# Prompt attention placed between the key chunks of sample attention in a two-layer decoder step on Trainium2

## The chip, the cores and the metric

The kernel runs on one core of a Trainium2 chip. A core has a matrix engine (PE, TensorE) with its weight loads (PEld), a vector engine (DVE), a scalar engine (ACT), GpSimd (POOL), a queue engine (SP), and 16 DMA engines. The engines run side by side, each through its own list of instructions in order, and wait for one another by semaphores. The metric is the device time of one execution in microseconds (us). All data are float32.

## The reference, cut to what matters

One inference step of two layers for a prompt of 512 tokens and, with the same weights, a sample group of 8 sequences with 4 new tokens each and 2048 past positions. In each layer:

```
x = x + 0.5 * SwiGLU_1(RMSNorm(x))
h = RMSNorm(x); z = h @ w_in             split into the heads of A, B and C
A: gated DeltaNet, 4 heads of 128
B: dilated sliding-window attention, 4 heads of 64, branches (128,1), (512,4), (2048,16)
C: differential attention, 4 heads: (softmax1 - lambda * softmax2) @ v, two 32-wide maps, 64-wide values
x = x + concat[A | B | C] @ w_out
x = x + 0.5 * SwiGLU_2(RMSNorm(x))
```

The prompt attends to itself (causal). For the samples C reads 2048 past keys and values per sequence from a paged pool by a page table, and B reads those of a window cache that its branches touch (896 of 2048 rows). A relative bias is added to every logit. Beside the outputs the step returns the new states, keys and values.

## The kernel before, in words

Activations stand transposed: 128 features on the partitions, 544 columns of tokens (512 prompt, 32 sample). A layer runs in stages: first FFN, input projection (`project`), DeltaNet for the prompt in four chunks (`chunk`) and for the samples (`sample_chunk`), `sample_attention`, `prompt`, output projection (`w_out`), second FFN. Each engine's order is written out by hand in its own block, and each block has a function of the same name for a stage; `s[...]` are semaphores, counted up over both layers. PSUM has 8 banks of 512 columns.

**Sample attention** (PE L908, ACT L1345, DVE L1928) goes through 46 key chunks of 512 KB (128 partitions x 4 rows x 256). Chunks 0 to 31 are of C, four sequences each in groups g = 0 and 1, gathered by POOL with indirect DMAs (`load_k`, L530); chunks 32 to 45 are of B, loaded by SP in four DMAs each. The ring for keys has 4 slots, and so has the ring for values (`load_v`, L538). Per chunk PE turns 8 blocks of 128 x 128 into banks 4 and 5 (`turn_keys`), ACT copies bank 4 (L1347) and DVE bank 5 (L1953) to the double-buffered `kt`, and PE multiplies the queries with it (`scores(n - 1)`, one chunk behind). The scores of a group fill banks 0 to 3; every fourth chunk DVE adds the bias and takes a partial maximum (`logits_c`). After 16 chunks follow the group's maximum, exponentials on ACT (`exp_c`), and weights: 17 matmuls of the exponentials with a matrix `comb`, which turn, normalise and combine the two maps (`weights_c`, L962). Then come the group's 16 value chunks, one per key chunk (`value`, L974), into banks 6 and 7; for group 0 from step 21, for group 1 from step 39, and its last ones after the key loop. `sums` (L994) collects the values over partitions. At the end B's window has its logits, maximum, exponentials, a diagonal matrix, weights and 16 value loads by SP.

**Prompt attention** (PE L1055, ACT L1390, DVE L2042) starts when DVE has copied out the samples' results. It has 16 units u: two heads times 128 queries, against 128 * (u % 4 + 1) keys; units 0 to 7 are of B with one map, 8 to 15 of C with two (`maps`). A unit is: scores (PE, L1067), logits with bias (DVE, L2051), maximum (L2056) and its negative (L2058), exponentials with row sums (ACT, L1398), reciprocals and weights (DVE, L2064 to L2075), turn of the weights (PE, `turned`, by the helper at L575), copy `p_pt` (ACT), values (PE, L1088), result (DVE, L2080). Engines work one to three units apart: PE's iteration u has scores of u + 1, turn of u - 1 and values of u - 2. Tiles and banks are those that sample attention has left: `p_s` and `p_pt` lie in `arena`.

**What stands around it.** SP loads the first two output-weight slots (L475, 1 MB each, into `weight_slots`) right after the input projection, then the four sample states (L370, needed by PE at L884), then B's keys and values. POOL writes out the four new sample states (L511) and then starts the gathers. The output projection (L1108) waits for the last prompt result, with all sample results in place before.

## Time and profile before

| | us |
|---|---|
| median of 3 runs | 3529.67 |
| lowest, highest | 3528.74, 3530.52 |
| the profiled execution | 3515.54 |
| its span, first to last instruction | 3513.9 |
| PE busy | 3117.7 (89%) |
| PEld busy | 2498.4 (71%) |
| DVE busy | 1597.9 (45%) |
| ACT busy | 623.5 (18%) |
| POOL busy | 143.8 (4%) |
| mean granted TensorE clock | 0.91 |

The profile is of one execution. A row of the timeline gives start and length in us, the engine, the line of the kernel, the operation with written and read tiles, a count if several were merged, and in brackets how long the engine had stood idle and what ended that.
### The profile page before, as it was taken

How to read it: one execution, taken by the hardware profiler on the slowest of the kernel's cores; microseconds unless marked ns; L12 is line 12 of the kernel's file. 1: busy time of each engine (PE TensorE's matmuls, PEld its weight loads, DVE VectorE, ACT ScalarE, POOL GpSimd, SP SyncE). 2: the span in 40 equal slices, each digit the busy share in tenths (PEclk: the TensorE clock that was granted, in tenths of full speed). 3: DMA queues.
4: the chain of work that ended last, by engine and by line, in shares of the span. 5: the costliest groups of instructions: out<-in, count | busy, mean ns of one | idle time of the engine just before them, and what ended most of it. 6: DMA issues, size and time to landing. Idle time of an engine off the chain costs nothing.

```text
span 3513.9 us, 46297 instructions
## 1 busy us (share of the span) xinstructions
PE 3117.7 (89%) x16564; PEld 2498.4 (71%) x16564; DVE 1597.9 (45%) x2966; ACT 623.5 (18%) x1233; POOL 143.8 (4%) x164
## 2 busy tenths in 40 slices
PE   2999999988887688999979999999878876899996
PEld 1788877877654366888868888788775534688885
DVE  3544535345443545445354454443554246444443
ACT  0111001233231321110011100122332213111100
POOL 0000000000052000000000000000003200000000
PEclk7999999999788588999989999999987867999998
DMA  4222232220079112221232212221005850232221
GB/s 142 61 84 72 66 90 60 66 70 0 27 270 268 39 60 60 84 84 57 75 87 84 84 57 78 69 72 60 28 27 181 242 153 1 84 84 84 60 75 59
DMA packets 363619, 299.01 MB, mean 85 GB/s; under 512 B 19426, under 2 KB 334972, under 8 KB 363170
## 3 DMA queue, kind: packets, MB, share of 16 engines
q1 hardware_dynamic: 340060, 213.88, 21.2%
q0 software_dynamic: 21888, 78.85, 6.7%
q10 hardware_dynamic: 1520, 4.27, 0.3%
q8 instruction: 94, 1.54, 0.2%
q14 instruction: 57, 0.47, 0.0%
HBM read 285.15 MB, written 11.81 MB: 85 GB/s over the span
## 4 chain that ended last, share of the span: by engine, by line
PE 80%; DVE 7%; DMA 6%; DVEq 2%; issue 2%; ACT 1%; ACTq 1%; SPq 1%; POOL 0%; POOLq 0%
PE banks L616 28%; PE banks L672 16%; PE banks L728 12%; PE banks L639 4%; PE banks L575 3%; PE banks L1108 3%; PE banks L802 1%; PE banks L810 1%; PE banks L814 1%; DMA hidden_or_projected<-in_cache_k,layer_cache_rows 1%; DMA arena<-in_cache_v,layer_cache_rows 1%; DMA arena<-in_cache_win_v 1%; DMA hidden_or_projected<-in_cache_win_k 1%; DVE arena L2056 1%; PE banks L904 1%
## 5 line engine op out<-in xcount | busy, mean ns | idle before, releaser
L728 PE MATMUL banks<-normed_or_mixed,weight_slots 128*128 128x272 f32 x1792 | 417.5, 395 | 10.5 <-DVE normed_or_mixed L1552 10.5
L728 PEld LDWEIGHTS banks<-normed_or_mixed,weight_slots 128*128 128x128 f32 x1792 | 343.0, 192 | 83.4 <-DVE normed_or_mixed L1552 12.0
L616 PE MATMUL banks<-arena 128*128 128x272 f32 x1408 | 347.8, 401 | 15.2 <-DVE arena L1577 15.2
L616 PE MATMUL banks<-normed_or_mixed,arena 128*128 128x272 f32 x1408 | 337.0, 392 | 0.0
L616 PEld LDWEIGHTS banks<-arena 128*128 128x128 f32 x1408 | 274.1, 195 | 76.0 <-DVE arena L1577 17.7
L616 PEld LDWEIGHTS banks<-normed_or_mixed,arena 128*128 128x128 f32 x1408 | 267.5, 190 | 55.1
L575 PE MATMUL banks<-constants,hidden_or_projected 128*128 128x128 f32 (+2 forms) x880 | 132.4, 300 | 61.8 <-DMA hidden_or_projected<-in_cache_k,layer_cache_rows 21.7
L672 PE MATMUL banks<-hidden_or_projected,keys_values_by_token 128*128 128x272 f32 x704 | 177.0, 392 | 0.0
L575 PEld LDWEIGHTS banks<-constants,hidden_or_projected 128*128 128x128 f32 (+2 forms) x880 | 105.6, 153 | 95.6 <-issue 78.1
L672 PE MATMUL banks<-hidden_or_projected,weight_slots 128*128 128x272 f32 x704 | 169.2, 392 | 0.0
L672 PE MATMUL banks<-arena,keys_values_by_token 128*128 128x272 f32 x704 | 169.2, 392 | 0.0
L575 PE MATMUL banks<-constants,arena 128*128 128x128 f32 (+4 forms) x306 | 62.2, 355 | 107.5 <-DVE arena L2075 46.0
L672 PEld LDWEIGHTS banks<-hidden_or_projected,keys_values_by_token 128*128 128x128 f32 x704 | 133.8, 190 | 27.6
L672 PEld LDWEIGHTS banks<-hidden_or_projected,weight_slots 128*128 128x128 f32 x704 | 133.8, 190 | 27.6
L672 PEld LDWEIGHTS banks<-arena,keys_values_by_token 128*128 128x128 f32 x704 | 133.8, 190 | 27.6
L1596 DVE TENSOR_TENSOR arena<-arena,banks 128x272 f32<-128x272 f32 x88 | 38.5, 437 | 249.9 <-PE banks L616 249.9
L639 PE MATMUL banks<-normed_or_mixed,keys_values_by_token 128*128 128x272 f32 x384 | 103.2, 415 | 43.5 <-DVE normed_or_mixed L1552 43.5
L1956 DVE COPY hidden_or_projected<-banks 128x512 f32<-128x512 f32 x92 | 63.6, 691 | 170.8 <-PE banks L575 170.7
L575 PEld LDWEIGHTS banks<-constants,arena 128*128 128x128 f32 (+4 forms) x306 | 44.7, 175 | 134.4 <-DVE arena L2075 57.6
L1179 ACT ACTIVATE arena<-banks 128x256 f32<-128x256 f32 (+7 forms) x164 | 83.0, 513 | 273.0 <-PE banks L802 107.2
L1108 PE MATMUL banks<-normed_or_mixed,weight_slots 128*128 128x272 f32 x512 | 122.0, 401 | 7.3 <-DVE normed_or_mixed L2131 6.3
L1734 DVE COPY hidden_or_projected<-banks 128x544 f32 x28 | 20.3, 724 | 222.7 <-PE banks L728 222.7
(365 smaller groups left out, 4631.0 us busy)
## 6 DMA issues: line engine op xcount, KB each, us to landing
weight_slots<-in_w_down SPq DMA_DIRECT2D x128, 256.0 KB
weight_slots<-in_w_in SPq DMA_DIRECT2D x28, 1024.0 KB
keys_values_by_token<-in_w_gate SPq DMA_DIRECT2D x48, 512.0 KB, 4.7
keys_values_by_token<-in_w_up SPq DMA_DIRECT2D x48, 512.0 KB, 4.7
weight_slots<-in_w_gate SPq DMA_DIRECT2D x40, 512.0 KB, 5.0
weight_slots<-in_w_up SPq DMA_DIRECT2D x40, 512.0 KB, 5.1
hidden_or_projected<-in_cache_win_k SPq DMA_DIRECT2D x112, 128.0 KB, 8.2
weight_slots<-in_w_down SPq DMA_DIRECT2D x64, 192.0 KB
```

Of the source, the lines that this page charges most:

```text
L575: return pe.transpose(out, in_, ident[0:rows, 0:rows])
L616: mm = pe.matmul(ps[:, bank, 0:HALF], weights[:, k, :], acts[:, k, :], start=first and k == 0, stop=k == 3, skip_group_check=True)
L639: mm = pe.matmul(ps[:, c, 0:HALF], one[:, k, :], hT[:, k, left], start=k == 0, stop=k == 3, skip_group_check=True)
L672: mm = pe.matmul(ps[:, bank, 0:HALF], weights[:, 128 * k:128 * k + 128], acts[:, k, :], start=j == 0 and k == 0, stop=j == 2 and k == n - 1)
L728: mm = pe.matmul(half(bank + 2 * u, h), wslot[:, slot, at:at + 128], hT[:, k, h * HALF:(h + 1) * HALF], start=k == 0, stop=k == KD - 1)
L802: mm = pe.matmul(ps[:, 4 if a else 7, 128 * i:128 * i + 128], m["LK"][:, 2 * a + i, :], m["T"][:, 2 * a + i, :], start=True, stop=True)
L810: mm = pe.matmul(ps[:, 2 + a, 128 * i:128 * i + 128], m["U"][:, 2 * a + i, :], m["M"][:, 2 * a + i, :], start=True, stop=True)
L814: mm = pe.matmul(ps[:, 5 + a, 128 * i:128 * i + 128], m["M"][:, 2 * a + i, :], m["U"][:, 2 * a + i, :], start=True, stop=True)
L1108: mm = pe.matmul(half(2 * (o % 4), h), wslot[:, o // 2 % 2, at:at + 128], hT[:, k, h * HALF:(h + 1) * HALF], start=k == 0, stop=k == KD - 1)
L1179: return act.activation(out, in_, ACT.Copy, scale=scale)
L1596: dve.tensor_tensor(x, one, a, ALU.add).then_inc(s["mix_out"], 1)
L1956: cp(kt[:, n % 2, 1, :], ps[:, 5, :]).then_inc(s["kt_v"], 1)
```

## The change

`sample_attention` and `prompt` become one function, `attention`, on each engine. The 46 key chunks are 46 steps, and after the samples' own work each step does a part of a prompt unit: `unit_at` gives units 0 to 7 two steps each (steps 0 to 15), units 8 to 15 three each (16 to 39); part 0 and 1 score the maps, the exponentials and weights of a unit come in the step after its last scores (part `maps(u)`), its turn in part 0 of the next unit and its values in part 1.

What else changes:
- ACT copies both banks of turned keys in one copy of 1024 columns; DVE's key copies are gone, with the signals `k_half`, `kt_a` and `kt_v`.
- Banks: turned keys 0 and 1, sample scores 2 only (four chunks at a time, so DVE's logits come every fourth chunk for B too), new scores and values 3, prompt scores 4 and 5, turned weights and results 6 and 7. DVE takes the maximum over all 2080 columns at once, without partial maxima.
- Group 0's values run in steps 20 to 35, copied out in two halves; group 1's in steps 38 to 45, two chunks per step, none after the loop. The sums of both groups come together after the windows' weights.
- `p_s` moves to the tile of the weight slots; so SP's first two output-weight loads move behind the last prompt turn and the first four window-value loads.
- POOL issues the first four key gathers before the four state stores.
- The output projection and the squares before it wait for the last sample results.

```diff
-        vblk = carve(work, 0, 8, 128)[0], carve(work, 1024, 8, 128)[0]
+        vblk = carve(work, RING * 1024, 8, 128)[0], carve(work, RING * 1024 + 1024, 8, 128)[0]
...
-        p_s, at = carve4(arena, 0, 2, 2, 2, SEQ)
-        p_pt, at = carve4(arena, at, 2, 2, 4, 128)
+        p_s, _ = carve4(raw[1], 0, 2, 2, 2, SEQ)
+        p_pt, _ = carve(work, 20 * NT, 2, 4, 128)
...
+        def unit_at(step):
+            if step < 16:
+                return step // 2, step % 2
+            return 8 + (step - 16) // 3, (step - 16) % 3
...
 @block.sync
-                for slot in range(2):
-                    sp.wait_ge(s["proj_done"], l * 28 + 26 + 2 * slot)
-                    load_wide(l, "w_out", slot * 256, slot)
                 sp.wait_ge(s["state_done"], l * 5 + 5)
...
                 for m in range(2 * NB_S):
+                    if m == RING:
+                        sp.wait_ge(s["ppt_mm"], l * 16 + 16)
+                        for slot in range(2):
+                            load_wide(l, "w_out", slot * 256, slot)
...
 @block.gpsimd
-                for h in range(NH):
-                    gp.wait_ge(s["st_new"], l * 4 + h + 1)
-                    st(O["delta_s"][ds(l, 1), :, h].rearrange("l b k v -> k (l b) v"), t["st"][:, h], "st_out")
...
+                gp.wait_ge(s["x_act"], l * 5 + 1)
+                for n in range(RING):
+                    load_k(n)
+                for h in range(NH):
+                    gp.wait_ge(s["st_new"], l * 4 + h + 1)
+                    st(O["delta_s"][ds(l, 1), :, h].rearrange("l b k v -> k (l b) v"), t["st"][:, h], "st_out")
+                for n in range(RING, CH_C):
                     load_k(n)
...
 @block.tensor
+                def prompt_scores(u, mp):
+                    hp, q0, wid = u // 4 % 2, 128 * (u % 4), 128 * (u % 4 + 1)
+                    if u:
+                        pe.wait_ge(s["p_log"], l * 24 + map_of(u, mp))
...
+                def prompt_turn(u):
+                    pe.wait_ge(s["p_soft"], l * 16 + u + 1)
+                    if u >= 1:
+                        pe.wait_ge(s["p_out"], l * 16 + u)
+                    if u in (8, 14):
+                        pe.wait_ge(s["pt_sb"], l * 3 + 1 + u // 14)
...
+                def prompt_step(step):
+                    u, part = unit_at(step)
+                    if part == 0:
+                        if u < 16:
+                            prompt_scores(u, 0)
+                        if 0 < u <= 16:
+                            prompt_turn(u - 1)
+                    if part == 1:
+                        if 8 <= u < 16:
+                            prompt_scores(u, 1)
+                        if 0 < u <= 16:
+                            prompt_values(u - 1)
...
+                for n in range(CH_K):
                     turn_keys(n)
+                    if n == 19:
+                        weights_c(0, 8)
+                    if n == 37:
+                        weights_c(1, 14)
+                    if n:
+                        scores(n - 1)
+                    if 20 <= n < 36:
+                        value(0, n - 20)
+                    if n >= 38:
+                        value(1, 2 * n - 76)
+                        value(1, 2 * n - 75)
+                    prompt_step(n)
...
 @block.scalar
                 def keys(n):
-                    act.wait_ge(s["k_half"], k_seen(l, n))
+                    act.wait_ge(s["k_free"], k_seen(l, n) + RING)
                     act.wait_ge(s["ks_mm"], l * CH_K + n + 1)
-                    copy(kt[:, n % 2, 0, :], ps[:, 4, :]).then_inc(s["kt_a"], 1)
+                    copy(kt[:, n % 2].rearrange("p a n -> p (a n)"), flat[:, 0:1024]).then_inc(s["kt_sb"], 1)
...
+                def prompt_step(step):
+                    u, part = unit_at(step)
+                    if u < 16 and part == maps(u):
+                        wid = 128 * (u % 4 + 1)
+                        act.wait_ge(s["p_max"], l * 16 + u + 1)
...
+                for n in range(CH_K):
+                    keys(n)
+                    if n in (17, 33):
+                        exp_c(n // 16 - 1)
...
+                    prompt_step(n)
...
 @block.vector
-                def keys(n):
-                    dve.wait_ge(s["k_free"], k_seen(l, n) + RING)
-                    dve.wait_ge(s["ks_mm"], l * CH_K + n + 1)
-                    cp(kt[:, n % 2, 1, :], ps[:, 5, :]).then_inc(s["kt_v"], 1)
...
                 def max_c(g):
                     dve.drain()
-                    dve.reduce_max(c_mx[:, g, 0:1], c_mx[:, g, 4:9], AX)
+                    dve.reduce_max(c_mx[:, g, 0:1], c_s[g][:, :], AX)
...
+                for n in range(CH_K):
...
+                    if 4 <= n <= CH_C and n % 4 == 0:
+                        logits(n // 4 - 1, n)
+                    if n == 40:
+                        logits(8, n)
+                    if n in (16, 32):
+                        max_c(n // 16 - 1)
+                    if n in (18, 34):
+                        comb_c(n // 16 - 1)
+                    prompt_step(n)
```

## Rows read from the trace of the kernel before

**Rows 1.** The chain that ended last, share of the span by engine (the page, part 4).

```profile
PE 80%; DVE 7%; DMA 6%; DVEq 2%; issue 2%; ACT 1%; ACTq 1%; SPq 1%; POOL 0%; POOLq 0%
```

**Rows 2.** Timeline: start us, length us, engine, line, operation. The stage's borders in both layers.

```profile
983.59 1.96 PE L575 MATMUL banks<-constants,hidden_or_projected 128*128 128x128 f32 x8 [2.30 <-ACT keys_values_by_token L1452]
...
1112.24 0.65 PE L958 MATMUL banks<-hidden_or_projected,arena 128*32 128x128 f32 x16
...
1167.11 2.98 PE L1067 MATMUL banks<-hidden_or_projected 64*128 64x128 f32 x12 [0.89 <-DVE normed_or_mixed L2038]
...
1260.24 5.76 PE L1108 MATMUL banks<-normed_or_mixed,weight_slots 128*128 128x272 f32 x24 [0.47 <-DVE normed_or_mixed L2080]
...
2680.03 1.96 PE L575 MATMUL banks<-constants,hidden_or_projected 128*128 128x128 f32 x8 [2.31 <-ACT keys_values_by_token L1452]
...
2967.64 5.76 PE L1108 MATMUL banks<-normed_or_mixed,weight_slots 128*128 128x272 f32 x24 [0.47 <-DVE normed_or_mixed L2080]
```

**Rows 3.** Stretches: us; PE, PEld, DVE, ACT, POOL busy; clock, DMA share, GB/s.

```profile
986.00:1028.00 42.00, 34.41 (x496) 25.87 (x496) 20.35 (x39) 14.91 (x23) 22.24 (x24) 0.95 0.81 286
...
1131.50:1167.10 35.60, 29.36 (x177) 11.71 (x176) 9.91 (x12) 1.94 (x2) 0.00 (x0) 0.53 0.58 177
...
1194.00:1254.00 60.00, 32.34 (x196) 20.87 (x194) 46.32 (x98) 26.26 (x77) 0.00 (x0) 0.62 0.00 1
```

**Rows 4.** Timeline, PE: one step with keys, scores and a value chunk.

```profile
1035.28 1.09 PE L575 MATMUL banks<-constants,hidden_or_projected 128*128 128x128 f32 x8
...
1037.31 1.09 PE L575 MATMUL banks<-constants,hidden_or_projected 128*128 128x128 f32 x8
```

**Rows 5.** Groups by form in layer 0's sample attention: count | busy us, mean ns | idle before.

```profile
L1179 ACT ACTIVATE hidden_or_projected<-banks 128x512 f32<-128x512 f32 x46 | 27.4, 596 | 82.1 <-PE banks L575 82.1
...
L1179 ACT ACTIVATE arena<-banks 128x1024 f32<-128x1024 f32 x6 | 6.0, 1022 | 38.3 <-PE banks L1049 27.6 <-PE banks L971 10.5 <-PE banks L990 0.2
...
L1956 DVE COPY hidden_or_projected<-banks 128x512 f32<-128x512 f32 x46 | 31.8, 691 | 79.9 <-PE banks L575 79.8
```

**Rows 6.** Timeline: exponentials of a narrow two-map unit, then logits to weights of a wide one.

```profile
1226.78 0.40 ACT L1398 ACTIVATE arena<-arena 128x128 f32<-128x128 f32 x1 [1.10 <-DVE arena L2058]
...
1243.83 2.35 DVE L2051 SCALAR_TENSOR_TENSOR arena<-banks,prompt_bias 128x1024 f32<-128x1024 f32 x2 [0.99 <-PE banks L575]
...
1246.27 2.29 DVE L2056 TENSOR_REDUCE arena<-arena 128x4 f32<-128x2048 f32 x1
...
1248.84 0.72 ACT L1398 ACTIVATE arena<-arena 128x512 f32<-128x512 f32 x1 [4.51 <-DVE arena L2058]
...
1251.16 1.54 PE L575 MATMUL banks<-constants,arena 128*128 128x128 f32 x6 [6.84 <-DVE arena L2075]
...
1251.80 0.18 DVE L2064 RECIPROCAL arena<-arena 128x4 f32<-128x4 f32 x1 [0.49 <-ACT arena L1398]
...
1253.15 1.41 DVE L2075 SCALAR_TENSOR_TENSOR arena<-arena 128x512 f32<-128x512 f32 x2
```

**Rows 7.** Timeline, PE: values of the widest unit and of the narrowest.

```profile
1189.28 1.09 PE L1088 MATMUL banks<-arena,keys_values_by_token 128*64 128x128 f32 x16
...
1193.17 0.44 PE L1088 MATMUL banks<-arena,keys_values_by_token 128*64 128x128 f32 x4
```

**Rows 8.** DMA issues of the stage: count, median us from issue to landing.

```profile
arena<-in_cache_v,layer_cache_rows POOLq DMA_INDIRECT x32, 7.2
```

**Rows 9.** Timeline: sample weights, the windows' diagonal, and 32 sums of values.

```profile
1090.07 3.76 PE L969 MATMUL banks<-arena 128*128 128x64 f32 x32
...
1116.99 0.29 DVE L2027 TENSOR_SCALAR arena<-constants,arena 128x128 f32<-128x128 f32 x1
...
1159.24 6.98 PE L1001 MATMUL banks<-constants,arena 128*128 128x16 f32 x32 [2.15 <-ACT arena L1179]
```

**Rows 10.** Stretches (columns as in rows 3): the state loads.

```profile
924.00:928.00 4.00, 4.00 (x39) 3.27 (x37) 0.89 (x6) 0.00 (x0) 0.00 (x0) 0.68 1.01 304
```

**Rows 11.** Timeline, PE: the products with the loaded states.

```profile
935.75 13.82 PE L884 MATMUL banks<-arena 128*128 128x8 f32 x64 [0.45 <-ACT arena L1179]
```

More of the change, by code:

```diff
@@ new lines, in prompt_turn @@
+                def prompt_turn(u):
[4 more added lines that the diff above has]
+                        pe.wait_ge(s["pt_sb"], l * 3 + 1 + u // 14)
+                        alone(pe)
+                    for kb in range(u % 4 + 1):
+                        cols = slice(128 * kb, 128 * kb + 128)
+                        for h2 in range(2):
+                            mm = turn(ps[:, 6 + h2, cols], p_s[:, u % 2, 0, h2, cols])
+                    mm.then_inc(s["ppt_mm"], 1)
@@ new lines, in prompt_values @@
+                def prompt_values(u):
+                    pe.wait_ge(s["ppt_sb"], l * 16 + u + 1)
+                    for kb in range(u % 4 + 1):
+                        for h2 in range(2):
+                            v0 = 128 * (u // 4) + 64 * h2
+                            mm = pe.matmul(ps[64 * h2:64 * h2 + 64, 6, 0:128], vtok[:, kb, v0:v0 + 64],
+                                           p_pt[:, h2, kb, :], start=kb == 0, stop=kb == u % 4)
+                    mm.then_inc(s["po_mm"], 1)
@@ L1152, in _ @@
                 alone(pe)
-                sample_attention(l)
-                prompt(l)
+                attention(l)
                 w_out(l)
@@ L1385, in sample_attention @@
-                values_c(1)
-                act.wait_ge(s["v_free"], l * 48 + 48 + RING)
-                copy(pv_b[:, 0:4, :], flat[:, 0:1024].rearrange("p (b n) -> p b n", b=4))
-                copy(pv_b[:, 4:8, :], flat[:, 3072:4096].rearrange("p (b n) -> p b n", b=4)).then_inc(s["pv_sb"], 1)
-            def prompt(l):
-                for u in range(17):
-                    if u < 16:
+                    copy(c_pt[:, g, 0:16, :], flat[:, 3072:4096].rearrange("p (k n) -> p k n", k=16))
@@ new lines, in prompt_step @@
+                def prompt_step(step):
+                    u, part = unit_at(step)
+                    if part == 0 and 2 <= u <= 8:
+                        prompt_result(u - 2)
+                    if part == 2 and 8 <= u <= 16:
+                        prompt_result(u - 1)
+                    if u < 16 and part < maps(u):
+                        prompt_logits(u, part)
+                        if part == maps(u) - 1:
+                            prompt_max(u)
+                    if u < 16 and part == maps(u):
+                        prompt_weights(u)
@@ new lines, in attention @@
+                for n in range(CH_K):
+                    if n == 2:
+                        dve.wait_ge(s["st_out"], l * 64 + 64)
+                        alone(dve)
+                        for g in range(2):
+                            new_logits(g, c_s[g][:, PAST:PAST + NS], scale_c, bias_cn[:, g, :])
+                        new_logits(2, b_s[:, KEYS_B:KEYS_B + NS], scale_b, bias_bn[:, :])
+                    if 4 <= n <= CH_C and n % 4 == 0:
[7 more added lines that the diff above has]
+                    prompt_step(n)
@@ new lines, in attention @@
+                for i in range(2):
+                    norm_a(i)
+                out_c()
+                for i in range(2, 4):
+                    norm_a(i)
+                dve.wait_ge(s["pv_mm"], l * 2 + 2)
+                for pair in range(2):
+                    for h2 in range(2):
+                        rows = slice(64 * h2, 64 * h2 + 64)
+                        at = 16 * pair + 4 * (2 * pair + h2)
+                        last = cp(hT[rows, 4 + pair, SEQ:NT].rearrange("p (b t) -> p b t", b=8),
+                                  ps[rows, 3, 0:256].rearrange("p (b x) -> p b x", b=8)[:, :, at:at + 4])
@@ L2091, in _ @@
+                last.then_inc(s["pv_out"], 1)
             with dve.Fori(0, DEPTH) as l:
@@ L2125, in _ @@
                 dve.drain()
-                sample_attention(l)
-                prompt(l)
+                attention(l)
                 for u in range(2):
```

363 lines of the change are left out of this document (129 added, 234 removed).

## The prediction

> **What bounds the kernel now.** I read first the chain that ended last: PE carries 80% of it [rows 1], so a change pays where PE is late or waits, and not where ACT or DVE is merely busy. Then I placed the changed stage by the timeline [rows 2]: in layer 0 the first key turn starts at 983.59 us, the last sample scores of the windows end at 1112.9, the prompt's first scores start at 1167.11 and the output projection at 1260.24. That is 276.7 us: 129.3 for 46 key chunks, 54.2 for the end of sample attention, 93.1 for the prompt. In layer 1 the same stage takes 287.6 us (2680.03 to 2967.64). Third, the busy time by stretches [rows 3]: over 42 us of the key chunks PE is busy 34.4 at clock 0.95, the 16 DMA engines are 81% busy, DVE is busy half the time and ACT a third; over 60 us of the prompt PE is busy 32.3, DVE 46.3, the DMAs nothing, and the clock is 0.62, that is, three quarters of it at the 1.2 GHz level. So one half of the stage leaves DVE and ACT free and the other leaves PE and the DMAs free; the change lays the one into the other.
>
> **What one step costs.** A step with keys, scores and one value chunk takes 2.03 us at the full clock (1035.28 to 1037.31) [rows 4]. Until now ACT and DVE each copied one bank of turned keys; now ACT alone copies both. 46 x 0.69 = 31.8 us leave DVE, and ACT's 27.4 us become 46 x 1.02 = 47 us [rows 5]. PE's turn of the next chunk waits for that copy: 1.09 + 1.02 and two hand-overs of 0.1 make 2.3 us the least step, hidden where the step's other PE work is longer.
>
> **Steps 0 to 15** (units 0 to 7, two steps each). PE has per unit 2 x (1.09 + 0.65) and gaps of 0.8, that is 4.3, and the unit's scores, turns and values: turns and values 1.09 each for the widest unit and 0.44 for the narrowest [rows 4, 7], the scores taken alike, so with the two widths between 3.1 for each kind over four units. Four units are 4 x 4.3 + 9.3 = 26.5, eight are 53, with the three products of new keys 55 us. Maxima, exponentials and weights of these one-map units are shorter (about 5 us even for the widest) and lie beside PE.
>
> **Steps 16 to 39** (units 8 to 15, three steps each). Here a ring of engines is longer than PE's work. From the end of one turn to the end of the next, widest unit: keys, scores and value of the next step 2.4 with gaps, scores of map two 1.1, their logits 1.2 (half of 2.35), maximum 2.3 and its sign 0.3, exponentials 3.0 (1248.84 to 1251.80), weights 2.8 (1251.80 to 1254.56) [rows 6], and the turn of the unit before, 0.9: 14.1 us with a hand-over or two. Narrowest: 2.4, scores 0.5, then not DVE's 1.5 but PE's old values, next turn and ACT's copy, 3.5, exponentials 1.7 (four of 0.39 and a read), weights 1.6, turn 1.1: 10.8 [rows 5 to 7]. By the same steps the two between take 10.4 and 12.0. Four units are 47.3, eight 95 us. Queued into that ring: the two sets of sample weights (17 matmuls, 3.8 us each on PE [rows 9] in front of a turn that also waits for ACT's copy; half is hidden, 4 us), and the maximum over 2080 columns, now taken at once (2.3 us by the widths of rows 6), with its exponential in ACT's queue ahead of a prompt unit, 3 us. 102 us.
>
> **Steps 40 to 45**, with two value chunks each. PE needs 3.9 us per step, but a step moves 1.57 MB, 5.5 us at the 286 GB/s of rows 3, and a value gather takes 7.2 us (median) to land in a ring of four [rows 8]. I take 32 us, near the transfers.
>
> **The end.** Before: 54.2 us. Window logits, maximum, exponential and diagonal took 4.4 (1112.9 to 1117.3) and take 4.1 with half of the logits done in step 40. Then come the weights, 3.8 as for the samples' and no longer behind late value chunks, the sums of both groups together, 7.0 [rows 9], and the window values with the last copies and sums, 35.6 at clock 0.53 [rows 3]. With 1.5 for hand-overs 52 us.
>
> **What moves for nothing.** Two loads of output weights, 2.1 MB or 7.3 us of transfer, go behind four window-value loads on SP. They pass 4 state loads, 56 window-key issues and 4 value issues. The wait on the last prompt turn ahead of them is over since step 40; behind it queue 12 value loads, first needed 15 us later, and that gap is the cover: without it, 7 us per layer. On POOL four key gathers pass the four state stores; their issue takes about 5 us from 924, and no store can start before PE's state products end at 949.6 [rows 11]. Fewer small maxima and one signal instead of two cost DVE nothing.
>
> **What moves at a price.** Those four gathers (2.1 MB) now start at 924, with the state loads, which fill the DMA engines over 924 to 928 (share 1.01) [rows 10]; PE needs the states at 935.75 [rows 11]. Bounds: 0 if the states go first, 3 us per layer if the two share alike (4.2 MB at 286 GB/s end at 938.7). I take 1, since the state loads are issued first. The Trainium skill (DMA: Bandwidth & Descriptors, the part on queues and rings) says that each engine takes packets from its queues in turn; by that rule it is the upper end, and the sum would be 4 us longer over two layers.
>
> **The clock.** The counts above are at the full clock. The key loop has 0.95, the prompt 0.62 [rows 3]. Between them I take 0.92, as PE is busy about 80% of the new ring: 16% of 189 us at the half level, where PE's work takes double, 15 us. Best 5 (clock 0.97), worst 70 (clock 0.62, all on the path).
>
> **The sum.** 55 + 102 + 32 + 52 + 15 + 1 = 257 us per layer, against 276.7 and 287.6: 19.7 and 30.6 less, 50 us in all. The profiled execution took 3515.54 us (span 3513.9, 1.6 around it), so it would take 3465; the median of the runs is 14.1 us higher, and from there it is 3480.
>
> **Rivals.**
> (a) *The ring runs clean.* Clock 0.97 and the last steps at PE's 23 us instead of 32: 257 - 10 - 9 = 238 per layer, 88 less: 3441. For it: at 82% busy PE kept 0.95. Against: the new ring leaves PE idle for 2 to 3 us in its wide units, which the key loop seldom does.
> (b) *The half clock.* Place: PE standing in front of the turn of a wide two-map unit until DVE's weights are done, about 3 us of idle time, eight units per layer. At clock 0.62 the sum is 257 - 15 + 70 = 312: 35 and 24 longer, 3589. It turns the sign where the clock costs 40 us instead of 15, a loop clock of about 0.79. For it: the prompt's own rows, where PE stood up to 6.8 us in front of such a turn [rows 6]. Against: now keys and values fill most of them. The Trainium skill (TensorE: Matmul & The Clock Gate, on oscillation) says that bursts of matmuls parted by waits fall back to the half clock again and again; by that rule it is this rival, and the prompt's rows agree while the key loop's don't.
> (c) *Nothing is hidden.* ACT works in order: a key copy stands behind exponentials, these behind a maximum, and each engine waits for the next, so that the prompt keeps its 93 us and the longer copies add 46 x 0.42 = 19 per layer: 3529.7 + 39 = 3568. Against: PE turns one chunk ahead of that copy.
> (d) *The transfers bound it.* 48 MB a layer (by the sizes of the chunks) at 286 GB/s are 168 us, below my 189 + 52, so this is only a floor and gets no chance.
>
> **How the numbers follow.** Forecast 0.50, (a) 0.22, (b) 0.14, (c) 0.14. The likeliest case's own range is 3455 to 3515 (10 us a layer on the ring, 5 on its last steps and the clock). Both signs hold weight, so the range reaches over (a) to 3435 and toward (c) to 3550; above it lie (b) and most of (c). 0.2% or 7 us is what a measurement of this kernel can tell. Faster: (a) and all but 0.02 of the forecast, 0.70. Slower: 0.24 of the 0.28 of (b) and (c), since a weak form of either ends at no change. Same: the 0.06 that is left.
>
> **What would show it.** In the timeline of the changed kernel: from the first key turn to the output projection 257 us in each layer; the 16th key turn 55 us after the first; from there to the 40th 102 us, with 14 us between the turns of the widest units; a full-clock step of 2.3 us where nothing of the prompt is in it; state products still starting at 936; clock over the loop at 0.92. Wrong if the narrow units also take 14 us (c), if the clock of the loop is below 0.8 (b), or if PE waits mostly for DMA in steps 16 to 39.

## The result and the profile after

The changed kernel takes 3425.62 us (median; 3424.5 to 3428.39), the kernel before took 3529.2 beside it: ratio 0.9707, 95% interval 0.969 to 0.9724, **103.6 us faster**. The forecast was 3480 and the range began at 3435. Direction right, gain twice what I said.

The profiled executions differ by less: 3515.54 before, 3428.39 after, 87.2 us by their spans. The page of the changed kernel, busy time by engine and, further down, the chain that ended last:

```profile
PE 3095.6 (90%) x16564; PEld 2494.0 (73%) x16564; DVE 1534.9 (45%) x2854; ACT 658.0 (19%) x1237; POOL 145.0 (4%) x164
...
PE 83%; DVE 7%; DMA 3%; ACT 2%; issue 2%; DVEq 2%; ACTq 1%; SPq 0%; POOL 0%; POOLq 0%
```

PE does almost the same busy time in a span 87 us shorter, and its share of the chain goes from 80% to 83%, DMA's from 6% to 3% [rows 1]. Line numbers have moved: L586 is the turn helper, L963 the sample scores, L997 the values, L1019 the prompt scores, L1111 the output projection. Timeline of PE, the stage's borders in layer 0 (first key turn, 17th, 41st, last scores, output projection), then layer 1's first and last:

```profile
991.66 1.97 PE L586 MATMUL banks<-constants,hidden_or_projected 128*128 128x128 f32 x8
...
1037.36 1.09 PE L586 MATMUL banks<-constants,hidden_or_projected 128*128 128x128 f32 x8
...
1141.42 1.09 PE L586 MATMUL banks<-constants,hidden_or_projected 128*128 128x128 f32 x8
...
1170.91 0.61 PE L963 MATMUL banks<-hidden_or_projected,arena 128*32 128x128 f32 x16
...
1222.56 3.08 PE L1111 MATMUL banks<-normed_or_mixed,weight_slots 128*128 128x272 f32 x6 [0.97 <-DVE normed_or_mixed L2080]
...
2650.61 1.97 PE L586 MATMUL banks<-constants,hidden_or_projected 128*128 128x128 f32 x8
...
2877.35 3.08 PE L1111 MATMUL banks<-normed_or_mixed,weight_slots 128*128 128x272 f32 x6 [0.96 <-DVE normed_or_mixed L2080]
```

The stage takes 230.9 and 226.7 us instead of 276.7 and 287.6 [rows 2]. The same pieces as in the sum of the prediction:

| piece, us | forecast | layer 0 | layer 1 |
|---|---|---|---|
| steps 0 to 15 | 55 | 45.7 | 45.7 |
| steps 16 to 39 | 102 | 104.1 | 100.7 |
| steps 40 to 45 and the last scores | 32 | 30.1 | 30.5 |
| end | 52 | 51.0 | 50.0 |
| clock, over all steps | 15 | in the above | in the above |
| state loads | 1 | (outside) | (outside) |
| sum | 257 | 230.9 | 226.7 |

The same pieces by stretches: from shortly before step 3's key turn to step 15, 16 to 39, 40 to 45, the end, and last steps 16 to 39 of layer 1 (us; PE, PEld, DVE, ACT, POOL busy; clock, DMA share, GB/s):

```profile
1000.00:1037.36 37.36, 35.05 (x453) 25.16 (x445) 22.51 (x54) 25.45 (x48) 16.64 (x18) 1.00 0.77 250
1037.36:1141.42 104.06, 88.02 (x1000) 60.19 (x999) 50.36 (x97) 52.67 (x102) 28.60 (x31) 0.92 0.72 209
1141.42:1171.50 30.08, 23.93 (x290) 15.63 (x286) 4.31 (x11) 10.81 (x17) 9.99 (x10) 0.83 0.89 275
1171.50:1222.56 51.06, 42.43 (x230) 22.64 (x227) 21.25 (x25) 4.68 (x9) 0.00 (x0) 0.52 0.58 168
...
2696.27:2796.92 100.65, 84.79 (x1000) 58.67 (x999) 50.39 (x97) 52.67 (x102) 28.74 (x31) 0.95 0.73 217
```

In the first piece PE is busy 94% at the full clock. In the second it is busy 85%, and DVE and ACT half the time each. What PE waits for there (engine, line, releaser: us in total, times, longest):

```profile
PE banks L586 <- DVE weight_slots L2024: 6.4, 4, 3.0
PE banks L586 <- DVE normed_or_mixed L2029: 4.0, 1, 4.0
PE banks L993 <- ACT hidden_or_projected L1181: 3.8, 1, 3.8
PE banks L586 <- ACT hidden_or_projected L1181: 1.0, 2, 0.5
PE banks L586 <- ACT arena L1181: 0.3, 1, 0.3
```

That is 15.5 of PE's 16.0 idle us: nine short waits for DVE and ACT, none for DMA. In the key loop of the kernel before PE waited 21.1 us for keys and values, here 3.5 us in all 46 steps of layer 0.

Of the 106.7 us that the stage saves (45.8 + 60.9), 19.5 are **given back** outside it: 8.1 ahead of layer 0's first key turn (983.59 to 991.66), 8.3 between the layers, 3.1 at the end. Two places can be read off; start, length, operation and idle time before it:

```profile
940.31 4.87 PE L895 MATMUL banks<-arena 128*128 128x8 f32 x22 [2.42 <-DMA arena<-in_state_delta]
...
990.65 1.08 PE L944 MATMUL banks<-hidden_or_projected,arena 128*32 128x32 f32 x64 [5.66 <-DVE arena L1944]
```

The state products wait 2.42 us for their loads (2.28 in layer 1), before 0.45 for ACT [rows 11]. And the scores of the new keys, which need DVE's `q_all`, now stand ahead of the first key turn, so PE waits 5.66 us where it waited 2.30 [rows 2]. A third is the output projection after layer 0, which comes out of a stretch at clock 0.52: its first 24 products take 8.63 us, before 5.76 [rows 2]. These three make 2.9 + 3.4 + 1.8 = 8.1 of the 8.3 us between the layers; Of layer 0's 8.1 us 2.6 lie ahead of the state products. 1.6 of them are already there at a product of the input projection (748.82 after, 747.19 before), whose place varies from 747.30 to 750.71 in the versions below though the code up to it is the same; 0.9 arise between that product and the samples' DeltaNet, in layer 0 only, and their cause is open. Of the 3.1 us at the end 1.5 are the output projection of layer 1, whose first 24 products take 7.28 us.

### The profile page after: what moved, and what is told of

It is laid out like the page before. It is cut to its first block, busy times and chain, and to the rows that moved or that the text cites. A ratio compares the mean times of both kernels' runs of the same rounds, so it can differ in the third digit from the quotient of the medians.

```text
span 3426.7 us, 45921 instructions
## 1 busy us (share of the span) xinstructions
PE 3095.6 (90%) x16564; PEld 2494.0 (73%) x16564; DVE 1534.9 (45%) x2854; ACT 658.0 (19%) x1237; POOL 145.0 (4%) x164
## 4 chain that ended last, share of the span: by engine, by line
PE 83%; DVE 7%; DMA 3%; ACT 2%; issue 2%; DVEq 2%; ACTq 1%; SPq 0%; POOL 0%; POOLq 0%
PE banks L627 29%; PE banks L683 16%; PE banks L739 12%; PE banks L650 4%; PE banks L586 4%; PE banks L1111 3%; PE banks L813 2%; PE banks L821 1%; PE banks L825 1%; ACT weight_slots L1376 1%; PE banks L963 1%; PE banks L915 1%; PE banks L1008 1%; PE banks L895 1%; DVE normed_or_mixed L1551 1%
## 5 line engine op out<-in xcount | busy, mean ns | idle before, releaser
L739 PEld LDWEIGHTS banks<-normed_or_mixed,weight_slots 128*128 128x128 f32 x1792 | 343.6, 192 | 83.6 <-DVE normed_or_mixed L1551 12.1
L1181 ACT ACTIVATE hidden_or_projected<-banks 128x1024 f32<-128x1024 f32 (+3 forms) x160 | 137.3, 864 | 243.6 <-PE banks L586 163.2
L586 PE MATMUL banks<-constants,hidden_or_projected 128*128 128x128 f32 (+2 forms) x880 | 136.8, 309 | 28.6 <-DMA hidden_or_projected<-in_x_sample 12.1
L586 PEld LDWEIGHTS banks<-constants,hidden_or_projected 128*128 128x128 f32 (+2 forms) x880 | 113.8, 160 | 48.3 <-issue 20.3
L1111 PE MATMUL banks<-normed_or_mixed,weight_slots 128*128 128x272 f32 x512 | 127.7, 414 | 8.3 <-DVE normed_or_mixed L2123 6.4
L1111 PEld LDWEIGHTS banks<-normed_or_mixed,weight_slots 128*128 128x128 f32 x512 | 103.0, 202 | 32.0 <-DVE normed_or_mixed L2123 7.2
L650 PEld LDWEIGHTS banks<-normed_or_mixed,keys_values_by_token 128*128 128x128 f32 x384 | 76.8, 201 | 64.3 <-DVE normed_or_mixed L1551 48.2
L1207 ACT ACTIVATE arena<-banks 128x272 f32<-128x272 f32 x88 | 34.9, 397 | 343.3 <-PE banks L650 343.1
```

The lines of the kernel that those rows point to most:

```text
L586: return pe.transpose(out, in_, ident[0:rows, 0:rows])
L650: mm = pe.matmul(ps[:, c, 0:HALF], one[:, k, :], hT[:, k, left], start=k == 0, stop=k == 3, skip_group_check=True)
L739: mm = pe.matmul(half(bank + 2 * u, h), wslot[:, slot, at:at + 128], hT[:, k, h * HALF:(h + 1) * HALF], start=k == 0, stop=k == KD - 1)
L1111: mm = pe.matmul(half(2 * (o % 4), h), wslot[:, o // 2 % 2, at:at + 128], hT[:, k, h * HALF:(h + 1) * HALF], start=k == 0, stop=k == KD - 1)
L1181: return act.activation(out, in_, ACT.Copy, scale=scale)
L1207: act.activation(p_one[:, g, :], ps[:, 3 * g, 0:HALF], ACT.Copy).then_inc(s["one_done"], 1)
```

## The experiments

Twelve kernels, in three groups of four with the kernel before beside each. Ratios are to that one; the changed kernel's own is 0.9707. Equal code differs between layers and runs: steps 16 to 39 take 100.7 to 104.1 us (mean 102.1; the changed kernel and the three whose edits lie outside, two layers each), the end 46.7 to 51.0. The clock of those eight stretches of steps 16 to 39 differs too, and with it goes the time: 104.1 us at 0.92, 102.1 to 103.2 at 0.93, 100.7 and 100.8 at 0.95. A piece is compared with these spreads.

**Prompt steps behind the key loop** (`e1_serial`).

```diff
                         value(1, 2 * n - 76)
                         value(1, 2 * n - 75)
+                for n in range(CH_K):
                     prompt_step(n)
```

(PE's part; ACT and DVE have the same. On PE the sample weights no longer wait for prompt results, ACT's last value copy comes ahead of its prompt steps, and DVE gets a wait of its own for the new scores.)

> The changed kernel with all 46 prompt steps taken out of the key loop and put behind it, in the same order; banks, single key copy, two values per step and the late sums stay. If laying the prompt into the key loop brings the gain: the stage (first key turn to output projection) is the bare loop, about 46 x 2.6 = 120 us, the prompt's old 93 and the end's 51, that is 264 against the 231 and 227 measured with the change: 33 to 37 more per layer, about 3495 us in all. Rival, that the rest of the change (one copy, group 1's values inside the loop, sums taken together) brings most of it: at most 10 more per layer, under 3446.

Measured 3639.34 us, ratio 1.0315 (1.029 to 1.0339): 214 us slower than the changed kernel and slower than the kernel before. Stretches: steps 0 to 15, 16 to 39, 40 to 45, then the prompt alone:

```profile
990.80:1029.70 38.90, 29.16 (x376) 21.69 (x368) 2.46 (x6) 16.39 (x16) 18.16 (x20) 0.89 0.74 246
1029.70:1119.80 90.10, 74.47 (x814) 52.85 (x814) 9.37 (x13) 33.06 (x35) 28.76 (x31) 0.81 0.81 243
1119.80:1149.00 29.20, 23.17 (x234) 12.63 (x230) 0.69 (x1) 6.16 (x7) 9.36 (x10) 0.71 0.89 253
1149.00:1280.00 131.00, 75.19 (x364) 41.82 (x368) 66.21 (x144) 40.11 (x114) 0.00 (x0) 0.54 0.07 21
```

Neither theory had this. The prompt part alone takes 131 us, not 93: PE waits 36.5 us for DVE's weights of two-map units, up to 8.2 us at a time. By the code the reason is that there is one bank pair for scores, one `p_pt` and one result bank, where the kernel before had two of each; no run takes these apart. The bare loop takes 158 us, before 129.3 (part of it eight value chunks that came later): PE's key turns wait 11.8 us for ACT's copy of both banks, before 1.2 us, and the clock is 0.81 and 0.71 there. Placed in the loop, the prompt costs 179.8 - 158.2 = 22 us. So the new layout makes each part slower on its own, by 38 and 29 us (the 29 with the eight chunks), and placing one in the other hides 109 of 131. It also keeps the clock up: 0.81 without the prompt in steps 16 to 39, 0.92 with it.

**Each prompt maximum twice** (`e2_max_twice`).

```diff
                     dve.reduce_max(p_mx[:, par, 0:2 * n], rows, AX)
+                    dve.drain()
+                    dve.reduce_max(p_mx[:, par, 0:2 * n], rows, AX)
```

> DVE takes each prompt maximum twice. Theory A, a ring of engines sets steps 16 to 39: all of the second maxima of the two-map units (0.69, 1.22, 1.75, 2.29 us, twice, 11.9) lie on it: 12 us more per layer there, 0 to 2 in steps 0 to 15, about 3450 us. Theory B, PE's own list sets them and only its few waits for DVE's weights (four in layer 0, 6.4 us) count: the repeats of just those units, about 6 per layer, 3438 us. If DVE is hidden altogether: 3426.

Measured 3478.36 us, ratio 0.9868 (0.9848 to 0.9888): 26 per layer. Steps 0 to 15 take 50.4, steps 16 to 39 121.7 and 120.7:

```profile
1040.90:1162.60 121.70, 98.39 (x1001) 68.08 (x999) 60.92 (x106) 53.07 (x102) 28.57 (x31) 0.82 0.61 179
```

DVE is busy 10.6 us more there and the stretch is 17.6 and 20.0 longer. The clock falls as well, from 0.92 and 0.95 to 0.82 and 0.84, and PE's busy time grows by 10.4 us in layer 0, so the 17.6 can't be divided for certain between DVE's work and PE's slower products. For a ring (theory A) speaks which units get longer: the rounds from one unit's turn to the next grow by 0.8 to 6.3 us, in all eight units of layer 1 and in seven of layer 0, not just in the four where PE had waited (theory B). Both theories missed the size, 12 and 6 us against 26 per layer, since neither had the clock, and steps 0 to 15 grow by 4.7 where A gave them 0 to 2.

**The sample score products twice** (`e3_scores_twice`).

```diff
-                    for pair in range(2):
-                        for b4 in range(4):
+                    for twice in range(2 if n < CH_C else 1):
+                        for pair in range(2):
+                            for b4 in range(4):
...
```

> PE does the sample score products of chunks 0 to 31 twice, 0.57 us more per chunk at the full clock. Both theories: 9 us more per layer in steps 0 to 15, where PE is busy 94%. Steps 16 to 32: theory A (ring), one of a unit's three scores lies on the ring, 3 us; theory B (PE's list), all of it, 9 us. Sum A 12 per layer, 3450 us; B 18 per layer, 3462 us.

Measured 3440.63 us, ratio 0.9763 (0.9743 to 0.9783). The added products are cheaper than I wrote: 32 instead of 16 records take 1.01 us to the next start where 16 took 0.57, so 0.44 per chunk. Steps 0 to 15 take 50.8 and 50.9, 5.1 more of 15 x 0.44 = 6.6: mostly PE's list, as both theories say. Steps 16 to 39 hold 17 x 0.44 = 7.5 of them (B) and take 106.1 and 104.6, 4.0 and 2.5 above the mean of equal code and 2.0 and 3.9 above the changed kernel's layers; A's share is 0.44 per unit of the first six, 2.6. Stretch of steps 16 to 39:

```profile
1040.20:1146.30 106.10, 94.24 (x1274) 67.87 (x1270) 50.75 (x97) 52.57 (x102) 28.43 (x31) 0.92 0.73 205
```

PE is busy 6.2 us more there, for 2 to 4 us of time, at clocks of 0.92 and 0.93. That is nearer to A's 2.6 than to B's 7.5: in steps 16 to 39 added work of PE costs a quarter to a half of its length, where DVE's 10.6 us above came with 17.6 and more.

**Two engines copy the turned keys** (`e4_two_copies`).

```diff
-                    copy(kt[:, n % 2].rearrange("p a n -> p (a n)"), flat[:, 0:1024]).then_inc(s["kt_sb"], 1)
+                    copy(kt[:, n % 2, 0, :], ps[:, 0, :]).then_inc(s["kt_sb"], 1)
```

```diff
                 for n in range(CH_K):
+                    dve.wait_ge(s["k_free"], k_seen(l, n) + RING)
+                    dve.wait_ge(s["ks_mm"], l * CH_K + n + 1)
+                    cp(kt[:, n % 2, 1, :], ps[:, 1, :]).then_inc(s["kt_v"], 1)
```

> The changed kernel with the copy of the turned keys divided as before: ACT one bank, DVE the other (0.60 and 0.69 us instead of 1.02 on ACT alone). Theory A: DVE's copies stand in the ring of the two-map units, one or two per unit, 8 us more per layer in steps 16 to 39, nothing in steps 0 to 15: 3442 us. Theory B: PE never waits long for the copy (2.1 us in all), so no change, 3422 to 3428. Below that if the single copy was a cost that the ring hid.

Measured 3431.9 us, ratio 0.9731 (0.9711 to 0.9751). Steps 0 to 15 take 47.6, 1.9 more in both layers, and steps 16 to 39 take 103.6 in both, inside the spread. Both expectations miss: the cost is where PE is busiest and not in the ring. In steps 0 to 15 of layer 0 PE waits 2.7 us for DVE's copies (seven times, up to 0.6 us), where it waited 1.1 us for ACT's. In steps 16 to 39 it waits 8.9 us for them, and less for DVE's weights (1.6 us instead of 6.4), so there the wait changed its place. The single copy brings about 2 us per layer in steps 0 to 15; the intervals of the two ratios overlap.

**Key gathers behind the state stores** (`e5_gathers_last`).

```diff
-                gp.wait_ge(s["x_act"], l * 5 + 1)
-                for n in range(RING):
-                    load_k(n)
                 for h in range(NH):
...
+                for n in range(RING):
+                    load_k(n)
```

> The changed kernel with POOL's first four key gathers back behind the four state stores. If the gathers ahead of the stores slow the state loads: the state products (L895 of the changed kernel) start without the 2.4 us wait for DMA in layer 0, and layer 1 likewise: up to 2.4 us less per layer, 3421 us. Rival: the gathers then land too late (the last is issued at 981 and takes 7 us, first key turn at 991.7, so 3 us to spare) and PE waits for keys in its first steps: 0 to 3 us more per layer, up to 3432 us. No change if the two cancel.

Measured 3415.8 us, ratio 0.9688 (0.9671 to 0.9705). The state products start without a wait for DMA:

```profile
937.58 12.75 PE L894 MATMUL banks<-arena 128*128 128x8 f32 x59 [0.45 <-ACT arena L1180]
```

and no turn of gathered keys waits for DMA, although the first four gathers are issued at 978 to 983; steps 0 to 15 take 44.8, 0.9 less, at clock 0.97 instead of 0.91. So the gathers ahead of the stores cost about 3 us per layer and bring nothing: 2 are the wait for the states, and why steps 0 to 15 gain too wasn't traced.

**Value copies one step earlier** (`e6_copies_early`).

```diff
-                    if n in (28, 36):
-                        values_c(0, (n - 28) // 8)
+                    if n in (27, 36):
+                        values_c(0, (n - 27) // 8)
...
-                    if n == 42:
+                    if n == 41:
                         values_c(1, 0)
```

> ACT copies out the first half of each group's values one step earlier (steps 27 and 41 instead of 28 and 42), ahead of a wide unit's four exponentials instead of behind them. PE stood 3.8 us in step 28 and 1.1 us in step 42 for these copies. Theory A (ring): the exponentials of unit 11 start when DVE's maximum is ready, so the copy moves into ACT's idle time; the wait goes, but the ring's next turn is at most 1 to 3 us earlier, since it waits for DVE's weights: 1 to 3 us less per layer, 3421 us. Theory B (PE's list): all 4.9 us per layer, 3416 us.

Measured 3425.19 us, ratio 0.9717 (0.9701 to 0.9734): no change. PE's timeline shows where the wait went:

```profile
1087.64 0.61 PE L993 MATMUL banks<-keys_values_by_token,arena 32*32 32x256 f32 x2
...
1092.82 1.97 PE L586 MATMUL banks<-constants,weight_slots 128*128 128x128 f32 x8 [3.58 <-DVE weight_slots L2024]
```

In the changed kernel PE stood 3.78 us in front of L993 and turned unit 11's weights at 1093.76 with no wait. Now it stands 3.58 in front of the turn, at 1092.82. The wait moved down the ring, as A says, but A's gain of 1 to 3 us isn't there.

**Idle products ahead of the waits** (`e7_filler`).

```diff
                 def prompt_turn(u):
+                    for _ in range({7: 24, 9: 6, 10: 12, 13: 20, 15: 10}.get(u, 0)):
+                        turn(ps[:, 7, 0:128], ident)
                     pe.wait_ge(s["p_soft"], l * 16 + u + 1)
```

> PE does 72 products that nothing uses (identity turns into bank 7, 0.13 us each at the full clock) just ahead of its waits for the weights of units 7, 9, 10, 13 and 15 (24, 6, 12, 20, 10 of them), so that it isn't idle there. Theory, the clock costs little because the ring is DVE's and ACT's: granted clock of steps 16 to 39 rises from 0.92 to 0.95 or more and the time changes by less than 2 us per layer, 3422 to 3430. Rival, the clock is on the path (my forecast's 15 us per layer): 4 to 6 us less per layer, 3415. If the products themselves delay a turn, 1 to 3 us more per layer.

Measured 3417.83 us, ratio 0.9698 (0.9679 to 0.9717). Steps 16 to 39 in layer 0:

```profile
1036.40:1135.10 98.70, 90.20 (x1064) 63.51 (x1060) 50.39 (x97) 52.71 (x102) 28.84 (x31) 0.97 0.77 220
```

The clock rises from 0.92 and 0.95 to 0.97 in both layers, and the stretch takes 98.7 and 98.8 us instead of 104.1 and 100.7, below all eight of equal code (mean 102.1 at a mean clock of 0.94). PE's nine waits there shrink from 15.5 to 8.1 us, as the products fill them. The time is 8 us below the changed kernel's by the medians and 3 by the ratios, whose intervals overlap; the stretches say 5.4 and 1.9 us, between my two expectations.

**Output weights behind all window values** (`e8_w_out_last`).

```diff
                 for m in range(2 * NB_S):
-                    if m == RING:
-                        sp.wait_ge(s["ppt_mm"], l * 16 + 16)
-                        for slot in range(2):
-                            load_wide(l, "w_out", slot * 256, slot)
...
+                sp.wait_ge(s["ppt_mm"], l * 16 + 16)
+                for slot in range(2):
+                    load_wide(l, "w_out", slot * 256, slot)
```

> SP issues the two loads of output weights (2.1 MB) behind all 16 window values instead of behind four. If they still have cover: they're issued when value 12 is used, about 12 us ahead of the output projection, and land in 8 us: no change, 3424 to 3428, and PE's waits for window values shrink by 1 us or so. If the cover is too short: up to 7 us per layer, 3439.

Measured 3420.79 us, ratio 0.9706 (0.9689 to 0.9722). The end takes 46.5 and 52.0, and the output projection waits 1.0 us for DVE as before, for no load. The loads have cover even there, so their move costs nothing, as forecast.

**Sums ahead of the windows' weights** (`e10_sums_gap`). The sums of both groups go into bank 3, ahead of the wait for the diagonal; the last sums then wait for DVE's copies.

```diff
+                for g in range(2):
+                    mm = sums(4, pv_c[g], 4, lambda b: b % 2, 3, 128 * g)
+                mm.then_inc(s["pv_mm"], 1)
                 pe.wait_ge(s["b_max"], l + 1)
```

> The sums of groups 0 and 1 (32 products, 7.0 us) go ahead of the windows' weights, into bank 3, where PE stood 3.9 us for DVE and ACT after the last scores. If PE's list bounds the end: sums and weights finish 3.2 us earlier (7.0 + 3.8 from 1172.6 on instead of 3.8 + 7.0 from 1175.4 on), 3 us less per layer. Rival, the window values are bound by their loads (16 loads, 7.3 MB, from 1163 on): PE then waits for DMA instead, 0 to 1 us less per layer. And if the clock stays at its upper level because PE isn't idle there, the windows' weights take 2.0 instead of 3.8 us and the values less than the 27 us that they took: up to 8 less per layer.

Measured 3414.19 us, ratio 0.9682 (0.9666 to 0.9698). The end takes 44.5 and 44.4 us, 6 less than the changed kernel's and 2 to 3 below the lowest of equal code; by the ratios the edit is worth 4 us per layer. PE before and after the edit:

```profile
1175.41 3.78 PE L1082 MATMUL banks<-arena,hidden_or_projected 128*128 128x128 f32 x16 [3.89 <-DVE arena L2069]
...
1179.69 7.01 PE L1008 MATMUL banks<-constants,hidden_or_projected 128*128 128x16 f32 x32
```

```profile
1166.61 3.75 PE L1008 MATMUL banks<-constants,hidden_or_projected 128*128 128x16 f32 x32 [0.28 <-ACT hidden_or_projected L1182]
1170.21 3.68 PE L1085 MATMUL banks<-arena,hidden_or_projected 128*128 128x128 f32 x16
```

The gap of 3.89 us is gone, and the sums, now straight behind the loop, take 3.75 instead of 7.01 us, at clock 1.00. The weights behind them still take 3.68 us: over 1170.20 to 1174.00 the clock is 0.55, although PE had stood idle for no more than 0.28 us just before. So the third expectation, that the upper level would hold, fails.

**Group 1's values one per step** (`e11_values_one`).

```diff
-                        value(1, 2 * n - 76)
-                        value(1, 2 * n - 75)
+                        value(1, n - 38)
...
                 scores(CH_K - 1)
+                for i in range(8, 16):
+                    value(1, i)
```

> Group 1's value chunks one per step from step 38 on, the other eight behind the last scores, as the kernel before had it. Theory, steps 40 to 45 are near the transfers: they take the same bytes, so the six steps get shorter by 6 value chunks (about 30 us now, 21 to 24 then) and the eight chunks behind the loop cost 8 x 1.1 to 1.8 us, that is 9 to 14: 0 to 5 us more per layer, 3426 to 3436. If two per step brought a gain by themselves: 8 us more per layer or over, 3441.

Measured 3429.48 us, ratio 0.9724 (0.9707 to 0.974). Steps 40 to 45 take 23.3, at 191 GB/s instead of 275, the end 59.1 and 60.6; together 82.4 and 84.0, against 81.1 and 80.4. Steps 38 and 39 are shorter too; the whole stage takes 228.2 and 229.7, against 230.9 and 226.7. Two per step bring nothing in the stage that stands out of the spread: work and bytes have to pass anyway.

**A version out of these** (`v2_best`, `v3_filled`): gathers behind the stores, value copies earlier, first key turn ahead of the new scores, sums ahead of the windows' weights; `v3_filled` with the idle products too.

> Four edits on the changed kernel: gathers behind the stores (measured alone), value copies one step earlier (measured alone), first key turn ahead of the new scores as in the kernel before, sums ahead of the windows' weights. Sum of the parts: 5 + 1 + 2 + 2 us per layer, 20 in all: 3405 us. If they share one slack: 3413.

> The same with the idle products ahead of PE's waits (92 of them, 20 more than alone, ahead of unit 11's turn). The filler alone took 2 to 5 us per layer out of steps 16 to 39, and their clock went from 0.92 to 0.97: 3 us less per layer than the version without, 3399 us. Rival: with the value copies earlier the waits are shorter and the products delay the turns: no gain or 2 us more per layer, 3405 to 3409.

Measured 3411.41 us, ratio 0.9664 (0.9648 to 0.968), and **3402.57 us, ratio 0.9638** (0.962 to 0.9656), the fastest of all, below the changed kernel's interval. Steps 16 to 39 of the latter:

```profile
1033.00:1130.80 97.80, 89.94 (x1084) 63.99 (x1080) 50.31 (x97) 52.84 (x102) 28.75 (x31) 1.00 0.80 224
```

At the full clock they take 97.8 and 96.1 us: the ring without any loss of clock. Without the idle products (`v2_best`) the same steps take 103.6 and 101.1 us at 0.90 and 0.93. The four edits bring 14 to 15 us together, less than the 20 of the sum; part of it is that the earlier first turn (985.51 in `v2_best`) is given back in steps 0 to 15 (47.1 instead of 45.7).

## Why the prediction was wrong in size

**The direction and the ring held.** I said that steps 16 to 39 are a ring of engines longer than PE's work, 102 us; they take 104.1 and 100.7, and PE waits in them for DVE and ACT, never for DMA. By units: the turns of units 8 to 15 start at 1057.43, 1067.54, 1079.26, 1093.76, 1105.79, 1117.89, 1133.30 and 1147.94. The rounds of 10.1, 11.7 and 14.5 us up to units 9, 10 and 11 stand against 10.4, 12.0 and 14.1; the last is 14.6. Those up to units 8, 12, 13 and 14 take 13.9, 12.0, 12.1 and 15.4 against 10.8, 10.8, 10.4 and 12.0, and there lie the sample weights and copies for which I had added 7 us. The doubled maximum and the doubled scores together show that DVE's links are on the path and that PE's own list is only in part. The narrow units do not take 14 (rival c), and the clock of the loop is 0.90 and 0.92, not under 0.8 (rival b).

**The clock term failed, 15 us.** The step was "PE is busy about 80% of the new ring: 16% of 189 us at the half level, where PE's work takes double, 15 us", added to everything. The mean clock was right (0.90 and 0.92 over all steps), but the price held in one piece only. In steps 16 to 39 the term's share is 8% of 102, 8 us. Measured, they take 97.0 us at 1.00 (`v3_filled`, mean of two layers; its other edits were worth nothing there by themselves), 98.8 at 0.97, 100.7 at 0.95 and 104.1 at 0.92. So the clock took 7 us in layer 0 and 4 in layer 1, nearly that share. PE is busy 3.2 us more in layer 0 than in layer 1 there and the stretch is 3.4 longer, with the same waits: the half level falls on products that the ring needs, right behind PE's waits:

```profile
1043.49 1.39 PE L586 MATMUL banks<-constants,weight_slots 128*128 128x128 f32 x8 [4.05 <-DVE normed_or_mixed L2029]
...
1044.67 1.92 PE L586 MATMUL banks<-constants,hidden_or_projected 128*128 128x128 f32 x8
...
1048.97 1.09 PE L586 MATMUL banks<-constants,hidden_or_projected 128*128 128x128 f32 x8
```

Of the other 7 us, charged to steps 0 to 15 and 40 to 45, little shows: the first take 45.7 us with their clock of 0.91 in it (44.8 at 0.97, in `e5_gathers_last`), the others 30.1 and 30.5 at 0.83, beside 28.5 at 0.88 and 29.2 at 0.94 in `e10_sums_gap`. And my 102, meant for the full clock, had 5 us too much in it, so that it stands near the measured times with their clock is luck.

The bounds of the term were reckoned too low. 189 us of work at a mean clock of 0.62, all on the path, take 305, which is 116 more and not 70; this makes rival (b) dearer and changes nothing in the result.

**Steps 0 to 15 failed, 55 instead of 45.7.** The step was "PE has per unit 2 x (1.09 + 0.65) and gaps of 0.8". PE's records overlap: a turn shown with 1.09 us is followed after 1.02, scores of 0.65 after 0.57. A bare chunk takes 1.6 us of PE, not 1.74, and there are next to no gaps (35.05 busy of 37.36 us at the full clock): steps 4 and 5 with unit 2's parts take 5.4 us where my count gives 6.5. The ends of matmuls in a profile are modelled; I added the lengths up as if they were measured.

**The last steps and the end held**: 30.1 and 30.5 for 32, at 275 GB/s, with 3.5 us of waits for value gathers in layer 0; 51.0 and 50.0 for 52. So did the zeros: the output weights have cover, and PE waits nowhere for the state stores.

**The state loads** cost PE 2.0 and 1.8 us, between my 1 and my upper bound of 3; that the gathers are the cause is shown by putting them back. The loads themselves were at that bound: their median time to landing was 9.0 us, and 6.0 with the gathers back behind the stores. The Trainium skill (DMA: Bandwidth & Descriptors, queues and rings) has an engine take packets from its queues in turn, which gives that upper end, and the 3.0 us of later landing agree with it.

**What I left out.** In the stage my sum was 26 and 30 us too long, 56 in all: 9 per layer in steps 0 to 15, 5 in the ring at the full clock, 8 and 11 in the clock term, the rest in small pieces. The 19.5 given back outside it pull the other way: beside the state loads, I priced neither the new scores ahead of the first key turn (3.4 us of PE idle per layer), a reordering that the code shows, nor the output projection's start at the half clock. That leaves 37 us, 3465 forecast for the profiled execution against 3428.39. The other 17 come from "the median of the runs is 14.1 us higher, and from there it is 3480": that held for the kernel before and not for the changed one, whose profiled execution lies 2.8 above its median.

**Rival (a)** came nearest, 238 per layer and 3441, though its first ground, a clock of 0.97, did not come true, nor did last steps of 23.

**Rival (b)** has a real mechanism, seen where it can't decide: with the prompt alone PE runs at 0.54, and longer maxima take steps 16 to 39 from 0.92 to 0.82, 7 to 9 us beyond the added work. The keys and values between keep it away. The Trainium skill (TensorE: Matmul & The Clock Gate, on oscillation) says that bursts of matmuls parted by waits fall back to the half clock again and again. Those two runs bear it out, and the change does in small: 0.92 and 0.95 in steps 16 to 39, with slow products behind the waits.

## What to carry to other kernels

Count PE's time by the distance between starts at the clock in question, not by adding the lengths of its records. Charge a lower clock piece by piece, and read from the rows where its slow products stand: in the ring a mean clock of 0.92 instead of 1.00 cost 7 us of 104, since they stood right behind PE's waits, on links that the ring needs; in the other pieces little of my flat 8% can be seen. And price a merge against the parts in their new layout: here each was slower alone, and only the overlap made the whole 3% faster.

## What the runs showed of the hardware

- Seventy-two idle products per layer, in places where PE would have waited, raised the granted clock of steps 16 to 39 from 0.92 and 0.95 to 0.97 (`e7_filler`). With 92 of them it was 1.00 (`v3_filled`), against 0.90 and 0.93 in the same version without (`v2_best`), and the steps took 97.8 and 96.1 us instead of 103.6 and 101.1.
- The same 32 sums of 16 columns took 7.01 us behind an idle gap of 3.89 us and the weights, and 3.75 us straight behind the key loop. Their place decided, not their work. The weights behind them ran at the half level all the same.
- Four gathers issued from 926.9 to 930.7, beside four state loads issued from 925.3 on another queue, raised the median time to landing of these from 6.0 to 9.0 us, and PE waited 2 us longer.
